# Queries and keys of a dilated attention: 512 moving columns, halves added on VectorE, rotary swaps on another queue

## The reference

```
hcat = (xn @ w_in).reshape(b, s, 3, 3, 16, 64)     # group; query, key, value; head; 64
q = apply_rope(hcat[:, :, :, 0], cos_f, sin_f)
k = apply_rope(hcat[:, :, :, 1], cos_f, sin_f)
v = hcat[:, :, :, 2]
return dilated_attention(q, k, v) @ w_o
# apply_rope: x1, x2 are the two halves of a head
return concatenate([x1 * c - x2 * s, x2 * c + x1 * s])
```

## Time and profile before

| | |
|---|---|
| Time, median of 3 runs | 1227.53 us (1226.71 to 1229.65) |
| The profiled execution | 1224.94 us, span 1223.1 us |
| TensorE, weight loads | busy 99%, 89% |
| VectorE, ScalarE, GpSimd | busy 67%, 52%, 17% |
| Granted TensorE clock | 0.998 of full speed |
| HBM | 169 GB/s over the span |
| A 1 MB load of this layer | 5.4 us from issue to landing, median |
| A swap's transfer of 64 KB | 3.9 us from issue to landing, median |

### The profile page before, as it was taken

The page is one execution under the profiler, slowest core; times in us unless marked ns, Lnnn a source line. Parts: engine busy times, 40 slices in busy tenths (PEclk is TensorE's granted clock), DMA queues, the critical chain, the costliest instruction groups (busy, mean ns, idle before and its releaser), DMA issues.

```text
span 1223.1 us, 19863 instructions
## 1 busy us (share of the span) xinstructions
PE 1212.0 (99%) x8225; PEld 1093.4 (89%) x8225; DVE 818.8 (67%) x1127; ACT 632.7 (52%) x813; POOL 204.5 (17%) x160
## 2 busy tenths in 40 slices
PE   8999999999999999999999999999999999999998
PEld 8988898888899989999998888898878899999986
DVE  6878768754475665776879854587875577656643
ACT  5575465534455454445555543456576545444342
POOL 2600010000011201110310000010010795443100
PEclk9999999999999999999999999999999999999999
DMA  9723456565676555554355656555554555555551
GB/s 235 261 84 124 139 173 196 182 204 176 206 228 203 175 180 178 188 176 147 104 170 175 195 185 206 175 185 172 173 172 138 167 187 181 173 173 181 198 182 60
DMA packets 162074, 214.27 MB, mean 175 GB/s; under 512 B 5260, under 2 KB 117199, under 8 KB 161983
## 3 DMA queue, kind: packets, MB, share of 16 engines
q1 hardware_dynamic: 156574, 205.11, 52.0%
q10 hardware_dynamic: 5216, 7.42, 2.1%
q0 software_dynamic: 192, 0.46, 0.1%
HBM read 205.63 MB, written 1.05 MB: 169 GB/s over the span
## 4 chain that ended last, share of the span: by engine, by line
PE 90%; DVE 4%; ACT 2%; issue 2%; DMA 2%; SPq 0%; POOL 0%; ACTq 0%; DVEq 0%
PE ps L538 61%; PE ps L553 8%; PE ps L556 4%; PE ps L628 4%; PE ps L570 4%; PE ps L725 3%; PE ps L762 2%; PE ps L733 2%; DVE wlo L1587 1%; DMA raw<-in_ev_w_in_dram 1%; ACT whi L1138 1%; DVE XT L1728 0%; DMA TB<-TA 0%; DVE SN L1659 0%; PE ps L1014 0%
## 5 line engine op out<-in xcount | busy, mean ns | idle before, releaser
L1587 DVE TENSOR_TENSOR wlo<-raw,whi 128x2048 fp32r<-128x2048 f32 (+1 forms) x167 | 385.9, 2312 | 194.0 <-ACT whi L1138 193.7
L1138 ACT ACTIVATE whi<-raw 128x2048 fp32r<-128x2048 f32 x188 | 358.0, 1907 | 200.1 <-PE ps L538 179.3
L538 PE MATMUL ps<-XHL,whi 128*128 128x256 f32 x1552 | 280.6, 284 | 0.0
L538 PEld LDWEIGHTS ps<-XHL,whi 128*128 128x128 f32 x1552 | 240.6, 192 | 0.6 <-issue 0.4
L538 PE MATMUL ps<-XHL,wlo 128*128 128x256 f32 x776 | 212.8, 283 | 0.1
L538 PE MATMUL ps<-whi,HL 128*128 128x512 f32 (+1 forms) x416 | 148.7, 373 | 0.0
L538 PE MATMUL ps<-whi,HH 128*128 128x512 f32 x384 | 147.2, 390 | 0.0
L538 PEld LDWEIGHTS ps<-XHL,wlo 128*128 128x128 f32 x776 | 145.7, 192 | 0.4 <-DVE wlo L1587 0.3
L538 PE MATMUL ps<-whi,XHL 128*128 128x512 f32 (+1 forms) x576 | 145.3, 345 | 0.0
L538 PE MATMUL ps<-wlo,HH 128*128 128x512 f32 x368 | 143.2, 389 | 0.0
L2316 POOL TENSOR_TENSOR wlo<-raw,whi 128x512 fp32r<-128x512 f32 x88 | 115.3, 1343 | 142.9 <-ACT whi L1138 142.7
(11 more groups left out here) (266 smaller groups left out, 1760.8 us busy)
## 6 DMA issues: line engine op xcount, KB each, us to landing
raw<-in_mlp_w_dram SPq DMA_DIRECT2D x64, 1024.0 KB, 5.2
raw<-in_od_w_in_dram SPq DMA_DIRECT2D x36, 1024.0 KB, 5.4
raw<-in_w_in_dram SPq DMA_DIRECT2D x24, 1024.0 KB, 5.1
raw<-in_w_ffn_gate_dram SPq DMA_DIRECT2D x12, 1024.0 KB, 5.2
raw<-in_w_ffn_up_dram SPq DMA_DIRECT2D x12, 1024.0 KB, 5.2
raw<-in_w_ffn_down_dram SPq DMA_DIRECT2D x12, 1024.0 KB, 5.1
TB<-TA ACTq DMA_DIRECT2D x96, 64.0 KB, 3.9
raw<-in_w_branch_dram SPq DMA_DIRECT2D x6, 1024.0 KB, 5.2
```

Of the source, the lines that this page charges most:

```text
L538: m = pe.matmul(to, l[c][a], r[c][b], start=first and k == 0, stop=last and k == 3 * n - 1)
L1138: act.activation(whi_of(n), raw_of(n), ACT.Copy, scale=1.0).then_inc(*tell(s_whi, ("whi", n)))
L1587: dve.tensor_tensor(wlo_of(n), raw_of(n), f32(whi_of(n)), ALU.subtract).then_inc(*tell(s_wlo, ("wlo", n)))
```

## The change

22 of the 24 qk slabs (all but the first two) are now computed by `beside`: 16 matmuls of 512 columns and 16 of 256 into two banks, where 48 of 256 went into one. ScalarE makes two copies of 128x256 to `TA`, VectorE two additions in place there, and the cosine product reads `TA`. The four swap transfers of all 24 slabs are issued by SyncE, each group right before the load of slab n + 5. For i below 6 the low weights' matmuls of both halves come last.

```diff
-            def beside(n, x, between=None):
+            def beside(n, x, late=False):
+                b = {}
+                w = [w_ready(n, 8, m * P, P) for m in range(2)]
+                def high(m):
+                    b[m] = bank(("beside", n, m))
                     for c in range(8):
...
+                        pe.matmul(b[m][:, :], w[m][c][0], XHL[:, c, :], start=c == 0, stop=False)
+                def low(m):
                     for c in range(8):
...
+                        i = pe.matmul(b[m][:, 0:S], w[m][c][1], x[c][0], start=False, stop=c == 7)
                     i.then_inc(*tell(s_product, ("product", "beside", n, m)))
+                high(0)
+                if not late:
+                    low(0)
+                high(1)
+                if late:
+                    low(0)
+                low(1)
...
                 elif kind == "qk":
                     if i > 1:
-                        (features_low_last if i < 6 else features)(n, x)
+                        beside(n, x, late=i < 6)
...
# ScalarE
-                b = take(("slab", n), [("rotated", swaps[0] - 2)] if swaps[0] > 1 else ())
-                act.activation(TA[k][:, :], b[:, :], ACT.Copy, scale=1.0).then_inc(*tell(s_act_out, ("copied", n)))
+                if i < 2:
+                    b = take(("slab", n))
+                    act.activation(TA[k][:, :], b[:, :], ACT.Copy, scale=1.0).then_inc(*tell(s_act_out, ("copied", n)))
+                else:
+                    copies(n, TA[k], ("rotated", swaps[0] - 2))
                 if 0 < i < EARLY - 1:
                     ahead(n + 1)
-                once.wait_ge(*at(("copied", n)))
-                for p in range(4):
-                    q = p ^ 1
-                    act.dma_start(TB[k][32 * p:32 * p + 32, :], TA[k][32 * q:32 * q + 32, :]).then_inc(
...
# VectorE
-                b = take(("slab", n), [("copied", n)])
-                dve.tensor_tensor(pair(QKV[hb % 3][3 * g + w]), pair(b[:, :]), twice(RP[:, 0:S]), ALU.mult).then_inc(
...
+                    v = TA[rotated[0] % 2]
+                    added(n, v, v, ("copied", n))
+                    dve.tensor_tensor(to, pair(v[:, :]), twice(RP[:, 0:S]), ALU.mult).then_inc(*tell(s_dve, ("scaled", n)))
...
# SyncE
+            def swap(k):
+                once.wait_ge(*at(("copied", turned_slabs[k])))
+                for p in range(4):
+                    q = p ^ 1
+                    sp.dma_start(TB[k % 2][32 * p:32 * p + 32, :], TA[k % 2][32 * q:32 * q + 32, :]).then_inc(
+                        *tell(s_swap[k % 2], *([("swapped", k)] if p == 3 else []), by=16))
             for n in range(7, SLABS):
+                if n - RAW in turned_slabs:
+                    swap(turned_slabs.index(n - RAW))
                 load(n)
```

More of the change, by code:

```diff
@@ L420, in ahead_of @@
             return [1, 2] if n == 0 else [n + 2] if n + 2 < SLABS else []
+        turned_slabs = [SLAB_ODD + i for i, (kind, *_) in enumerate(DILATED) if kind == "qk"]
         pieces = {s: [(k, j) for k in range(3) for j in range(4)][max(0, s - 22) if s > 23 else 0:s - 21] for s in range(23, 34)}
@@ L540, in product @@
                     m.then_inc(*tell(s_product, event))
-            def beside(n, x, between=None):
[L545 to L549, removed]
+            def beside(n, x, late=False):
[3 more added lines that the diff above has]
+                    b[m] = bank(("beside", n, m))
                     for c in range(8):
-                        for event in (w[c][2], x[c][2], x[c][3]):
+                        for event in (w[m][c][2], x[c][2], x[c][3]):
                             once.wait_ge(*at(event))
-                        pe.matmul(b[:, :], w[c][0], XHL[:, c, :], start=c == 0, stop=False)
+                        pe.matmul(b[m][:, :], w[m][c][0], XHL[:, c, :], start=c == 0, stop=False)
+                def low(m):
                     for c in range(8):
-                        once.wait_ge(*at(w[c][3]))
-                        i = pe.matmul(b[:, 0:S], w[c][1], x[c][0], start=False, stop=c == 7)
+                        once.wait_ge(*at(w[m][c][3]))
+                        i = pe.matmul(b[m][:, 0:S], w[m][c][1], x[c][0], start=False, stop=c == 7)
                     i.then_inc(*tell(s_product, ("product", "beside", n, m)))
+                high(0)
[5 more added lines that the diff above has]
+                low(1)
                 released[n] = [("product", "beside", n, 1)]
@@ L1707, in attend, with added @@
                     outputs(group_of(first + s - 3))
-            def added(n, to, copy):
+            def added(n, to, copy, *events):
                 for m in range(2):
@@ L1713, in added @@
                     v = slice(m * S, m * S + S)
-                    dve.tensor_tensor(to[:, v], b[:, 0:S], copy[:, v], ALU.add).then_inc(*tell(s_dve_out, ("taken", "beside", n, m)))
+                    dve.tensor_tensor(to[:, v], b[:, 0:S], copy[:, v], ALU.add).then_inc(*tell(s_dve_out, ("taken", "beside", n, m), *(events if m else ())))
                 once.wait_ge(*at(("taken", "beside", n, 1)))
@@ L1959, in rotate @@
                     once.wait_ge(*at(("sine", k)))
-                    once.wait_ge(*at(("taken", "slab", SLAB_ODD + DILATED.index(("qk", hb, g, w)))))
+                    once.wait_ge(*at(("scaled", turned_slabs[k])))
                     dve.tensor_tensor(dst, dst, TB[k % 2][:, :], ALU.add).then_inc(*tell(s_dve, ("odd", hb, g, w), ("rotated", k)))
@@ L1980, in odd_slab @@
                     once.wait_ge(*at("rp"))
-                b = take(("slab", n), [("copied", n)])
-                dve.tensor_tensor(pair(QKV[hb % 3][3 * g + w]), pair(b[:, :]), twice(RP[:, 0:S]), ALU.mult).then_inc(
-                    *tell(s_dve_out, ("taken", "slab", n)))
+                to = pair(QKV[hb % 3][3 * g + w])
+                if i < 2:
+                    b = take(("slab", n), [("copied", n)])
+                    dve.tensor_tensor(to, pair(b[:, :]), twice(RP[:, 0:S]), ALU.mult).then_inc(
+                        *tell(s_dve_out, ("taken", "slab", n), ("scaled", n)))
+                else:
+                    v = TA[rotated[0] % 2]
+                    added(n, v, v, ("copied", n))
+                    dve.tensor_tensor(to, pair(v[:, :]), twice(RP[:, 0:S]), ALU.mult).then_inc(*tell(s_dve, ("scaled", n)))
                 if i >= EARLY:
```

1 line of the change is left out of this document (removed).

## The result

| | before | after |
|---|---|---|
| Median (lowest to highest), 18 runs each | 1225.33 us (1222.99 to 1229.65) | 1229.99 us (1228.78 to 1231.91) |
| Ratio after / before, 95% interval | | 1.0040 (1.0031 to 1.0049) |
| The profiled execution, its span | 1224.94, 1223.1 | 1231.91, 1230.1 |

The account below looks back on a forecast made before the run. The prediction took a closed circle of VectorE and ScalarE to replace TensorE as the bound in the dilated attention steps. Its terms, 0.1 + 10.2 - 1.6 + 0.8 = +9.5 us on 1227.53, gave 1237.0, range 1229.0 to 1242.0.

Parts of the forecast that it names:

- The bound and the additions: Dilated attention steps: two VectorE additions cost 0.80 us a slab, and the bound moves from TensorE to VectorE and ScalarE.
- The circle of VectorE and ScalarE: Attention steps: minimum, exponential, high part, low part, cosine product, next minimum; 14.36 us a pair, becoming 15.96 without collisions.
- The collisions: Attention steps: GpSimd's sine product and VectorE's low part or cosine product wait for each other, 1.2 us a pair (0.7 to 1.7).
- a landing of 2.7: Swap on SyncE's queue: transfers land 2.7 us after issue, so the sine product starts 4.0 after the next minimum.
- The rule on who excludes whom: A VectorE instruction with two SBUF inputs and a GpSimd one reading SBUF exclude each other throughout, whoever starts first.
- the second rival: Attention steps: the sine product meets neither VectorE operation; about +2 us, 1229 to 1230.5, chance 0.17.
- the main case: Whole kernel: VectorE and ScalarE become the bound, with additions and collisions; +9.5 us, own range 1233.5 to 1240.5, chance 0.63.
- The loads: Ten early slabs: loads wait behind swaps on SyncE's queue; priced at nothing, with 1 us of loss as bound.
- The saving of 0.8 on the early slabs: Early slabs, TensorE: wide matmuls save 0.16 us on each of 5 slabs, and this saving stays.
- The sum: Whole kernel: 0.1 + 10.2 - 1.6 + 0.8 = +9.5 us, giving 1237.0.
- the 1.6 in hand: Second stretch, step 19: 1.6 us of slack before TensorE's values matmuls, taken off the +10.2.
- the twelfth slab: End of the second stretch: this slab adds 1.4 us, for which 0.6 more is in hand, so +0.8.

Follow-up runs that it names:

- e4: The changed kernel with GpSimd's sine product cut to one column of each half; 1225.31 us against 1223.93 before, ratio 1.0007.
- e8: The changed kernel with the sine product cut to one column of each half and a third VectorE addition of 128x256; 1230.02 us against 1224.83 before.
- e2: The changed kernel with the swaps back on ScalarE's queue, waiting for VectorE's second addition; 1238.58 us against 1223.93 before, ratio 1.0114.
- e11: The changed kernel with each load on SyncE's queue issued ahead of the swap; 1228.21 us against 1223.72 before, ratio 1.0032.
- e9: The changed kernel once more, unaltered; 1229.86 us against 1224.83 before, ratio 1.0042.
- e6: The changed kernel with additions, cosine product and rotation moved to the next step, ahead of VectorE's low part; 1219.76 us against 1224.83 before, ratio 0.9959.
- e7: The changed kernel without the two additions per slab and with the sine product cut to one column of each half; 1219.75 us against 1224.83 before.
- e3: The changed kernel without VectorE's additions, ScalarE's copies kept; 1226.74 us against 1223.93 before, ratio 1.0018.

## Why the prediction was half right

**The bound and the additions: right.** The circle of VectorE and ScalarE became the bound, and every slab paid the additions (forecast 0.80, and 15.96 for the pair without collisions; e4 15.95, e8 0.33 for each further addition). Of the +7.4 from step 9 to step 19 they are 4.18 (79.76 less 75.58; forecast 4.2). The wide slab takes what the MLP's did: two halves from 385.06 to 390.64 in this chain of the changed kernel, 5.58, against 5.59.

```profile
385.06 1.84 PE ps L556 x8
...
390.64 1.08 PE ps L738 x12
```

**The collisions: the step that failed.** "With the same issue time, and a landing of 2.7 as no load is under way then (bounds 2.0 and 3.2)" put the sine product 4.0 after the minimum and priced a pair at 1.2. It came 2.7 after the minimum in the steady part, so that it cleared the even steps' low parts wholly and the odd steps' but for 0.41; it never reached the cosine product. Five pairs cost 3.2 (after less e4), not 6.0, and a pair came to 16.36, not 17.2. The 2.7 was too near its source: I had 3.05 from rows 3 and 5 and took off a little for the load. What a load does to these transfers could be read beside it. The GB/s of the DMA engines between 500 and 525 us (40 slices of 0.625 us), in before:

```profile
GB/s 0 0 97 292 377 382 316 392 213 30 0 0 92 321 385 377 374 359 190 10 16 0 0 0 0 31 157 378 388 359 365 316 92 23 0 36 231 369 387 367
```

and in after:

```profile
GB/s 102 56 190 377 390 374 302 10 0 0 23 105 102 105 87 161 347 393 413 316 48 11 13 43 102 105 102 80 200 354 387 387 315 25 0 0 0 105 105 105
```

In before the swap was issued from 508.38 on, right as the engines filled with a load (508 to 512, up to 385 GB/s). In after its four transfers stand alone as the stretch at about 105 GB/s (from 506.9), and the load comes behind them. Alone, a transfer lands 2.0 after its issue, and the sine product starts 1.5 after the last issue's end. The prediction's lower bound of 2.0 was still above that. That it is the load and not the queue is shown by both queues: ScalarE's has 2.0 alone and 4.9 beside a load (e2), SyncE's 2.0 alone and 3.9 beside one (e11), and 4.8 in after itself for the early swap issued from 351.79, right behind the load of 351.17.

The Trainium skill, "SBUF — State Buffer", section "The DMA setup-cost knee", puts a transfer at about 2 us plus its bytes at 436 GB/s, an estimate of 2.15 for 64 KB. The 2.0 of after agrees; the 3.9 of before, a median of 2.0 to 5.5, shows that this doesn't hold beside a load.

The rule on who excludes whom held in the traces read here: low part, cosine product and sine product waited for each other nearly in full (3.31, 1.78, 3.44), and whoever was first kept its time. Only the moment at which they meet was mistaken. So the second rival (0.17) was nearer than the main case in price: no collisions would have been +2, the measured +4.7 lies between it and +9.5. With the collisions taken away, as in e4, the rest of the sum holds: +1.4 by the medians and +1.65 in the layer.

**The loads: within the bound, at its bad end.** Priced at nothing, with 1 us of loss as bound; TensorE's idle time there is 0.86, and the sign that the prediction named for it (TensorE idle for a low part before 390 us) did show. The chain of the changed kernel shows the path, the first swap's issues and then the load behind them:

```profile
350.53 0.59 SPq L2501
...
351.17 6.64 DMA raw<-in_od_w_in_dram
...
357.83 1.93 ACT whi L1151
...
359.85 2.30 DVE wlo L1598
...
365.41 2.30 DVE wlo L1598
...
367.76 17.30 PE ps L541 x142
```

ScalarE's high part waited for the load that had stood behind the swap, and TensorE for the low part that followed. The saving of 0.8 on the early slabs is eaten. The prediction said that this saving stays, but its sum has no term for it; the two omissions cancel.

**The sum.** From the layer's start, step 9's minimum is 1.0 later than before (141.96 against 140.95; forecast 0), step 9 to 19 adds 7.4 (forecast 10.2), and the rest of the layer takes 1.2 off (forecast -0.8, with the 1.6 in hand): 7.2. The error is in the collisions at both places, with opposite signs. In the long stretch they cost 2.8 less than priced. Up to step 9 they cost 1.9 (141.96 against e4's 140.06) where 0.8 was priced, and that is why step 9 comes late; it isn't the early loads, for e4 has these too (TensorE idle for 0.66 before 391 us) and reaches step 9 0.9 earlier than before. In the whole layer the collisions are 5.55 (289.20 less 283.65), where the terms of the prediction add up to some 7.4 (0.8, 6.0 and 0.6 for the twelfth slab).

**What stays open.** Both profiled executions of the changed kernel have a layer 7.0 to 7.2 us longer, and e9's profiled execution was 1230.74; the medians differ by 4.7 and 5.0. So of the 4.8 us between the forecast rise and the measured one the trace accounts for about half (9.5 less 7.2), and the other half lies between the profiled executions and the medians: its cause is open. The profiled execution of before lies 0.4 under its median, and after's is the highest of its 18 runs. Outside the layer, too, the profiled executions of all kernels here differ by up to 2.3 us (span less layer: 939.06 in e6, 941.34 in e7, 941.1 in before). Executions of one kernel may differ in which of the first low parts collide, as e11 and after do by 1.5 us; no trace of a faster execution of the changed kernel was taken, so this is argued and not shown.

## What to carry to other kernels

An engine at two thirds of its time can be the bound when its work stands in a closed circle with another; measure the circle from one minimum to the next, and put new work where the engine waits in it, not behind the last operation ahead of the next turn: the same change costs 0.4% with its additions in one place and gains 0.4% with them in the other. Where two engines exclude each other, half a microsecond in the second one's start counts (0.6 us more made 1.0 us of a collision of 0.4), so take its duration from a row with the same neighbours on the DMA engines, or carry its bounds as a range. And an ablation that shifts the timing of what remains (e3) prices nothing by itself; pair it with the one that takes the other suspect away.

## What the runs showed of the hardware

- A 64 KB transfer from SBUF to SBUF lands 2.0 us after its issue when alone, whichever of the two engines issues it, and 3.9 to 4.9 beside a 1 MB load (medians: 3.9 in before, 3.9 in e11, 4.9 in e2). An issue takes 0.6 on either engine's queue.
- Four issues hold ScalarE for 2.44 us that its busy time doesn't count; the bracket of the next row puts the wait down to the engine whose semaphore came last (e2).
- A collision costs whoever comes second nearly all that is left of the first: 0.41 and 1.02 for a low part, 1.1 for a cosine product, up to 2.1 for a sine product (3.44 less 1.3).
